# Three RMS norms in a two-block layer kernel: row factors applied behind the linear units, two norms merged into one factor, first units paired

## What is computed

```python
def rms_norm(x, g):
    y = x32 * lax.rsqrt(jnp.mean(x32 * x32, axis=-1, keepdims=True) + RMS_EPS)
    return (y * g.astype(jnp.float32)).astype(x.dtype)
...
    h = rms_norm(x, b_norm[j])                      # norm 1
    z = h @ w_in                                    # short_conv_mix
    c, b, u, g = jnp.split(z, 4, axis=-1)
    cu = c * u
    ...                                             # conv: 3 causal taps a channel
    y = b * conv * jax.nn.silu(g)
    x = x + y @ w_out
    x = rms_norm(x, final_norm)                     # norm 2
...
    h = rmsnorm(x, norm_mix_pre)                    # norm 3
    proj = jnp.einsum('bsd,de->bse', h, w_in)       # GLU, q, k, v, two gates
    ...
    mix = jnp.einsum('bsd,de->bse', merged, w_out)
    x = x + rmsnorm(mix, norm_mix_post)             # norm 4
    h = rmsnorm(x, norm_ffn_pre)                    # norm 5
    gu = jnp.einsum('bsd,df->bsf', h, w_ffn_up)
    gate, up = jnp.split(gu, 2, axis=-1)
    ff = jnp.einsum('bsf,fd->bsd', jax.nn.silu(gate) * up, w_ffn_down)
    x = x + rmsnorm(ff, norm_ffn_post)              # norm 6
```

## Time and profile before

| | us |
|---|---|
| median of 3 runs | 2272.75 |
| lowest, highest | 2270.09, 2278.52 |
| the profiled execution, its time | 2277.93 |
| the profiled execution, its span | 2276.2 |
| TensorE busy in the span | 2088.7 |
| DVE busy | 1405.7 |
| ACT busy | 992.6 |
| GpSimd busy | 279.1 |

### The profile page before, as it was taken

One profiled execution on the slowest core, in us unless ns is written; L12 is line 12 of the kernel. 1 busy time (PEld: TensorE's weight loads), 2 busy tenths in 40 slices (PEclk: granted clock), 3 DMA queues, 4 the chain that ended last, 5 costly groups with the idle time before them and its releaser, 6 DMA issues.

```text
span 2276.2 us, 43064 instructions
## 1 busy us (share of the span) xinstructions
PE 2088.7 (92%) x16752; PEld 1651.1 (73%) x16752; DVE 1405.7 (62%) x2178; ACT 992.6 (44%) x1742; POOL 279.1 (12%) x241
## 2 busy tenths in 40 slices
PE   6999999888888888989999999788989989999998
PEld 4877777677777766768788878566755757787876
DVE  7778888766666634465544555599765655434345
ACT  6666666455566653232322232411565334323233
POOL 4120000012222321000000000297000000000000
PEclk9999999899999988999999999999999999999998
DMA  4445555733332222323333333122211222333332
GB/s 115 125 138 170 174 170 171 200 71 87 69 78 69 69 76 59 94 69 101 88 97 93 92 101 92 47 74 65 84 38 38 80 68 75 100 93 92 93 88 79
DMA packets 395949, 215.16 MB, mean 95 GB/s; under 512 B 85136, under 2 KB 374312, under 8 KB 395816
## 3 DMA queue, kind: packets, MB, share of 16 engines
q1 hardware_dynamic: 395608, 213.18, 32.4%
q10 hardware_dynamic: 208, 0.06, 0.0%
HBM read 181.68 MB, written 31.52 MB: 94 GB/s over the span
## 4 chain that ended last, share of the span: by engine, by line
PE 69%; DVE 17%; ACT 8%; issue 5%; SPq 1%; DMA 1%; ACTq 0%; DVEq 0%
PE bank L1613 18%; PE bank L1614 17%; PE bank L1615 17%; PE bank L546 3%; DVE dconv L2104 3%; DVE w_lo L1834 2%; PE bank L523 1%; ACT w_hi L1337 1%; PE bank L554 1%; PE bank L455 1%; PE bank L497 1%; PE bank L469 1%; DVE tmp L1852 1%; PE bank L476 1%; DVE xh L1839 1%
## 5 line engine op out<-in xcount | busy, mean ns | idle before, releaser
L1613 PE MATMUL bank<-xl,w_hi 128*128 128x512 f32 x1680 | 670.6, 399 | 27.1 <-DVE xl L1839 9.9
L1614 PE MATMUL bank<-xl,w_lo 128*128 128x512 f32 x1680 | 661.4, 394 | 0.0
L1615 PE MATMUL bank<-xl,w_hi 128*128 128x512 f32 x1680 | 660.8, 393 | 0.0
L1337 ACT ACTIVATE w_hi<-w_raw 128x1024 fp32r<-128x1024 f32 x280 | 294.2, 1051 | 449.2 <-PE bank L1615 448.4
L1834 DVE TENSOR_TENSOR w_lo<-w_raw,w_hi 128x1024 fp32r<-128x1024 f32 x280 | 346.2, 1237 | 116.6 <-ACT w_hi L1337 107.6
L1613 PEld LDWEIGHTS bank<-xl,w_hi 128*128 128x128 f32 x1680 | 317.3, 189 | 129.3 <-issue 34.1
L1615 PEld LDWEIGHTS bank<-xl,w_hi 128*128 128x128 f32 x1680 | 317.6, 189 | 71.0
L1614 PEld LDWEIGHTS bank<-xl,w_lo 128*128 128x128 f32 x1680 | 317.9, 189 | 65.3
L1613 PE MATMUL bank<-xh,w_hi 128*128 128x512 f32 x480 | 202.1, 421 | 40.0 <-DVE w_lo L1834 23.7
L1614 PE MATMUL bank<-xh,w_lo 128*128 128x512 f32 x480 | 193.3, 403 | 0.0
L1615 PE MATMUL bank<-xh,w_hi 128*128 128x512 f32 x480 | 192.7, 402 | 0.0
(11 more groups left out here) (334 smaller groups left out, 3089.7 us busy)
## 6 DMA issues: line engine op xcount, KB each, us to landing
w_raw<-in_a_w_in SPq DMA_DIRECT2D x64, 512.0 KB, 4.3
w_raw<-in_b_w_in SPq DMA_DIRECT2D x64, 512.0 KB, 4.1
w_raw<-in_w_ffn_up SPq DMA_DIRECT2D x44, 512.0 KB, 3.9
w_raw<-in_w_in SPq DMA_DIRECT2D x36, 512.0 KB, 3.8
w_raw<-in_a_w_out SPq DMA_DIRECT2D x16, 512.0 KB, 4.1
w_raw<-in_b_w_out SPq DMA_DIRECT2D x16, 512.0 KB, 4.0
w_raw<-in_w_ffn_down SPq DMA_DIRECT2D x16, 512.0 KB, 4.1
d_g<-sq SPq DMA_DIRECT2D x16, 256.0 KB, 2.3
```

Source lines behind the costliest of these rows:

```text
L1337: A(w_hi[0:rows, slot, 0:nkb, 0:ncol], w_raw[0:rows, slot, 0:nkb, 0:ncol], ACT.Copy).then_inc(s_hi, 1)
L1613: mm(outp, wh, xlo, start=start, stop=False)
L1614: mm(outp, wl, xhi, start=False, stop=False)
L1615: return mm(outp, wh, xhi, start=False, stop=stop)
```

## The change

Norm 1: the high and low halves of x are made from x times the gain alone, in the eight units before the norm (`even` gets `hi` and `low`), and the factor r of each token is applied behind the units: r squared to the product c times u by way of c, r inside the sigmoid of g, r squared on g times b. The mean matmul stands behind the first convolution unit.

Norms 2 and 3: beside the sum of squares (`acc`), DVE sums the squares weighted with `square_gain` = final gain squared + 1e-6 (`acc2`). With an epsilon of 1e-12 its mean gives the product of both norms' factors at once, and the GLU's input is made with it and the product of both gains. The residual itself gets its final norm later: eight products `final_norm` in the first two GLU turns. The first two GLU units are interleaved part by part (`two_units`).

Norms 4 and 5: after the residual add, x times gain is split directly; the factor of norm 5 is applied in the FFN turns, in place of in front of them. Its squares are summed by TensorE between the matmuls of the first two FFN units, which are interleaved too.

The high and low panels of the second unit behind boundaries 2 and 3 are made ahead of the norm, and the first turns of two loops are written out. The core of the diff (each piece moved left by its common indentation):

```diff
@@ -1347,19 +1357,22 @@
-def norm(n, x, ready=None):
+def norm(n):
+
...
-    o(A(rstd[:, 0, :], bank[4][:], ACT.Ln, bias=eps[:, 0:1]))
-    A(rstd[:, 1, :], rstd[:, 0, :], ACT.Exp, scale=-0.5).then_inc(s_rs, 1)
+    if n == 3:
+        o(A(acc[:], bank[5][:], ACT.Ln, bias=eps[:, 0:1]))
+        A(acc[:], acc[:], ACT.Exp, scale=-0.5).then_inc(s_rs, 1)
+        return
+    e = 3 if n == 2 else 0
+    o(A(rstd[:, 0, :], bank[4][:], ACT.Ln, bias=eps[:, e:e + 1]))
+    ins = A(rstd[:, 1, :], rstd[:, 0, :], ACT.Exp, scale=-0.5)
+    if n in DEFERRED_SQUARED:
+        ins = A(rstd[:, 0, :], rstd[:, 0, :], ACT.Exp, scale=-1.0)
+    ins.then_inc(s_rs, 1)
@@ -1499,39 +1512,52 @@
-                act.wait_ge(s_sqa, 2 * t + (n * DK + u - 1))
+                if hi is not None:
+                    A(hi[:, 0, bass.ds(2 * t + u, 1), :], x[:, bass.ds(2 * t + u, 1), :], ACT.Copy,
+                      scale=col(gain, 2 * t + u)).then_inc(s_xhi, 1)
+                act.wait_ge(s_sqa, 2 * t + (squares(n) + u - 1))
                 A(sq[:, u, :], x[:, bass.ds(2 * t + u, 1), :], ACT.Square).then_inc(s_sq, 1)
...
-even(U_OUT1 + DK, DK // 2, xT2, 1)
-norm(1, None)
-for k in range(DK):
-    x_high(X_H2 + k, xl[2][:, 0, k, :], k % 2)
+even(U_OUT1 + DK, DK // 2, xT2, 1, hi=xl[2], gain="b_norm")
...
+            if first and u == 0:
+                norm(1)
...
-                sigmoid(gate3[:]).then_inc(s_sc, 1)
+                sigmoid(gate_z[:]).then_inc(s_sc, 1)
...
-norm(2, None)
-norm(3, xT2, lambda k: (s_xn, k + 1))
+ahead(U_GLU, 2, 0, 0)
+norm(2)
 for k in range(DK):
     x_high(X_H3 + k, xh[:, 0, k, :], k % 2)
+norm(3)
...
@@ -1579,27 +1605,39 @@
-norm(4, None)
-
-norm(5, xT2, lambda k: (s_mg, k + 1))
+ahead(U_FFN, 2, 0, 0)
+norm(4)
+
 for k in range(DK):
-    x_high(X_H4 + k, xl[0][:, 0, k, :], k % 2)
+    act.wait_ge(s_mg, k + 1)
+    A(xl[0][:, 0, k, :], xT2[:, k, :], ACT.Copy, scale=col("norm_ffn_pre_2", k)).then_inc(s_xhi, 1)
+    act.wait_ge(s_sqa, squares(5) + k - 1)
+    A(sq[:, k % 2, :], xT2[:, k, :], ACT.Square).then_inc(s_sq, 1)
+norm(5)
...
+    def ffn(t, first=False):
+        if not first:
+            ahead(base, 2, t, 0)
+        else:
+            ahead(base, 2, t, 1)
...
+        sigmoid(tmp[:, 1, :]).then_inc(s_us, 1)
...
@@ -1628,13 +1666,12 @@
-    if n not in SUMMED_BY_PE:
-        pe.wait_ge(s_sqa, (n + 1) * DK)
-        mm(bank[4][:], mean_d[:], acc[:], start=True, stop=True).then_inc(s_ms, 1)
+    if n == 2:
+        pe.wait_ge(s_sqb, DK + 1)
     else:
-        for k in range(DK):
-            pe.wait_ge(s_sq, n * DK + k + 1)
-            mm(bank[4][:], mean_d[:], sq[:, k % 2, :], start=k == 0, stop=k == DK - 1).then_inc(s_sqa, 1)
+        pe.wait_ge(s_sqa, squares(n + (n != 3)))
+    mm(bank[5 if n == 3 else 4][:], mean_d[:], acc2[:] if n == 2 else acc[:], start=True,
+       stop=True).then_inc(s_ms, 1)
@@ -1756,14 +1795,36 @@
-norm(1)
-    phase(base, 4, KB, xl[2], X_H2)
+    phase(base, 4, KB, xl[2], X_H2, then=None if half else lambda: norm(1))
 norm(2)
 norm(3)
-phase(U_GLU, 2, CT + 3 * AT // 2, xh, X_H3)
+
+def two_units(base, x, ready, total=None):
+
+    order = [(0, 0)]
+    for k in range(1, DK - 2):
+        order += [(0, k), (1, k - 1)]
+    order += [(0, DK - 2), (0, DK - 1)] + [(1, k) for k in range(DK - 3, DK)]
+    for u, k in order:
+        if k == 0:
+            pe.wait_ge(s_lo, base + u + 1)
+            pe.wait_ge(s_free[u], base // 2)
+        if u == 0:
+            pe.wait_ge(s_xlo, ready + k + 1)
+        last = three(bank[u][:], w_hi[:, u, k, :], w_lo[:, u, k, :], x[:, 0, k, :], x[:, 1, k, :],
+                     k == 0, k == DK - 1)
+        if k == DK - 1:
+            last.then_inc(s_unit, 1)
+        if total is not None:
+            if u == 0 and k:
+                total(k - 1)
+            elif (u, k) == (1, DK - 3):
+                total(DK - 1)
+two_units(U_GLU, xh, X_H3)
+phase(U_GLU, 2, CT + 3 * AT // 2, xh, X_H3, started=True)
@@ -1809,10 +1870,15 @@
-norm(5)
+def total_square(k):
+
+    pe.wait_ge(s_sq, squares(5) + k + 1)
+    mm(bank[4][:], mean_d[:], sq[:, k % 2, :], start=k == 0, stop=k == DK - 1).then_inc(s_sqa, 1)
+two_units(U_FFN, xl[0], X_H4, total_square)
...
-    phase(base, 2, n, xl[0], X_H4)
+    phase(base, 2, n, xl[0], X_H4, started=part == 0)
@@ -2021,9 +2080,20 @@
+            if low is not None:
+                part = bass.ds(2 * t + u, 1)
+                dve.wait_ge(s_xhi, 2 * t + (x0 + u + 1))
+                V.scalar_tensor_tensor(out=low[:, 1, part, :], in0=where, scalar=col(gain, 2 * t + u),
+                                       in1=low[:, 0, part, :].bitcast(F32), op0=ALU.mult,
+                                       op1=ALU.subtract).then_inc(s_xlo, 1)
...
+                if n == 2:
+                    dve.wait_ge(s_sqb, 2 * t + (u + 1))
+                    V.scalar_tensor_tensor(out=acc2[:], in0=sq[:, u, :],
+                                           scalar=square_gain[:, bass.ds(2 * t + u, 1)], in1=acc2[:],
+                                           op0=ALU.mult, op1=ALU.add).then_inc(s_sqb, 1)
...
-    even(U_OUT1 + half * DK, DK // 2, xT2, True, n=1 if half else None)
+even(U_OUT1, DK // 2, xT2, True)
+even(U_OUT1 + DK, DK // 2, xT2, True, n=1, low=xl[2], gain="b_norm", x0=X_H2)
...
-dve.wait_ge(s_xlo, X_H2)
-norm(1, "b_norm", split(X_H2, xl[2], DK), xT2, summed=True)
...
+o(V.tensor_tensor(both_gains[:], gain_f, gain_m, ALU.mult))
+o(V.tensor_tensor(square_gain[:], gain_f, gain_f, ALU.mult))
+o(V.tensor_scalar(square_gain[:], square_gain[:], RMS_EPS, None, ALU.add))
@@ -2056,7 +2130,8 @@
-        V.tensor_copy(c_sb[:], bank[0][:]).then_inc(s_free[0], 1)
+        dve.wait_ge(s_rs, 1 + NT)
+        V.tensor_tensor(c_sb[:], bank[0][:], rr_b, ALU.mult).then_inc(s_free[0], 1)
@@ -2070,23 +2145,32 @@
-        V.tensor_scalar(gate3[:], bank[0][:], CLAMP, None, ALU.max).then_inc(s_zc, 1)
-        dve.wait_ge(s_sc, ct + 1)
-        V.tensor_tensor(gate3[:], gate3[:], bank[0][:], ALU.mult).then_inc(s_free[0], 1)
+        o(V.tensor_tensor(gate_z[:], bank[0][:], r_b, ALU.mult))
+        V.tensor_scalar(gate_z[:], gate_z[:], CLAMP, None, ALU.max).then_inc(s_zc, 1)
+        V.tensor_tensor(gate3[:], bank[0][:], rr_b, ALU.mult).then_inc(s_free[0], 1)
         dve.wait_ge(s_free[0], 2 * t + (base // 2 + 2))
         o(V.tensor_tensor(gate3[:], gate3[:], conv3[:, 0, :], ALU.mult))
+        dve.wait_ge(s_sc, ct + 1)
+        o(V.tensor_tensor(gate3[:], gate3[:], gate_z[:], ALU.mult))
         w_low(n0 + 4, 0)
         dve.wait_ge(s_unit, n0 + 4)
         V.tensor_tensor(tmp[:, 0, :], gate3[:], bank[1][:], ALU.mult).then_inc(s_free[1], 1)
         x_low(t + (X_YC + KB * half), xl[half][:, 1, bass.ds(t, 1), :], xl[half][:, 0, bass.ds(t, 1), :], 0)
-    repeat(dve, KB, conv, o, 4)
+    repeat(dve, KB, conv, o, 6)
+    if half:
+        V.memset(acc2[:], 0.0).then_inc(s_sqb, 1)
-norm(2, "final_norm", lambda k, scaled: scaled(xT2[:, k, :]).then_inc(s_xn, 1), xT2,
-     summed=True)
+w_low(U_GLU + 1, 1)
-norm(3, "norm_mix_pre_2", split(X_H3, xh, DK), xT2)
+norm(2, lambda k: both_gains[:, k:k + 1], split(X_H3, xh, DK), xT2)
+
+def final_norm(k):
+
+    dve.wait_ge(s_rs, 3 + NT)
+    V.scalar_tensor_tensor(out=xT2[:, k, :], in0=xT2[:, k, :], scalar=col("final_norm", k), in1=acc[:],
+                           op0=ALU.mult, op1=ALU.mult).then_inc(s_xn, 1)
@@ -2115,6 +2200,8 @@
+    for k in range(4 * j, 4 * j + 4 if j < 2 else 0):
+        final_norm(k)
@@ -2205,36 +2292,57 @@
...
-    norm(n, gain, step, src, summed=True)
-residual(4, "norm_mix_post_2", mixed, s_mg)
-
-
-norm(5, "norm_ffn_pre_2", split(X_H4, xl[0], DK), xT2)
+        if low is not None:
+            for m in ([k - 2] if k >= 2 else []) + ([k - 1, k] if last else []):
+                low(m)
+def ffn_low(k):
+
+    dve.wait_ge(s_xhi, X_H4 + k + 1)
+    V.scalar_tensor_tensor(out=xl[0][:, 1, k, :], in0=xT2[:, k, :], scalar=col("norm_ffn_pre_2", k),
+                           in1=xl[0][:, 0, k, :].bitcast(F32), op0=ALU.mult,
+                           op1=ALU.subtract).then_inc(s_xlo, 1)
+w_low(U_FFN + 1, 1)
+dve.wait_ge(s_xn, DK)
+residual(4, "norm_mix_post_2", mixed, s_mg, ffn_low)
...
         n0 = 2 * t + base
-        w_low(n0 + 1, 1)
+        if not first:
+            w_low(n0 + 1, 1)
         dve.wait_ge(s_unit, n0 + 1)
-        V.tensor_scalar(rstd[:, 0, :], bank[0][:], CLAMP, None, ALU.max).then_inc(s_ug, 1)
+        dve.wait_ge(s_rs, 5 + NT)
+        V.tensor_tensor(rstd[:, 0, :], bank[0][:], r_ffn, ALU.mult).then_inc(s_free[0], 1)
+        dve.wait_ge(s_free[0], t + (base // 2 + 1))
+        V.tensor_scalar(tmp[:, 1, :], rstd[:, 0, :], CLAMP, None, ALU.max).then_inc(s_ug, 1)
         w_low(n0 + 2, 0)
+        o(V.tensor_tensor(rstd[:, 0, :], rstd[:, 0, :], r_ffn, ALU.mult))
         dve.wait_ge(s_us, t + (j0 + 1))
-        V.tensor_tensor(rstd[:, 0, :], rstd[:, 0, :], bank[0][:], ALU.mult).then_inc(s_free[0], 1)
```

(3 more changed lines are left out.)

102 lines of the change are left out of this document (61 added, 41 removed).

## The result

| | before | after |
|---|---|---|
| median of the runs | 2273.67 us (4 runs) | 2243.98 us (4 runs) |
| ratio, 95% interval | | 0.9869 [0.9845, 0.9893] |
| profiled execution (span) | 2277.93 (2276.2) | 2241.48 (2239.8) |

The forecast was 2243.0. On another chip the changed kernel took 2245.06 us against 2278.70: 0.9858 [0.9836, 0.9881].

What follows compares the result with a forecast made beforehand. TensorE, busy 92% of the span, was taken as the bound away from stage boundaries, so only its waits could be saved. Savings of 11.4 + 13.6 + 1.7 + 1.9 + 1.1 = 29.7 us gave a 2243 us median; profiled 2248, range 2236 to 2257.

Steps and rivals of the forecast that it cites:

- Boundary 1: Norm 1, before the convolution: splitting x no longer waits for rstd; saves 11.4 us (10.3 to 11.6).
- Boundary 2: Norms 2 and 3, before GLU: one chain goes; 13.6 us saved (11.5 to 15.5). E: end of the last unit before.
- Half clock: TensorE's restarts after idle run at half clock: 1.7 us added before GLU, 1.5 before the FFN.
- payback of 0.5 for the final norm: First two GLU turns: the eight final-norm products moved there cost 0.5 us in all (0 to 2.5).
- Rival (d): GLU stage: the final norm's eight products (5.4 us) come back whole, 2248 us; forecast with this included, 0.83.
- Boundary 3: Norms 4 and 5, before the FFN: mean matmuls between paired units make TensorE the bound; saves only 1.7 us (-2 to 4).
- the new wait: Third FFN unit: its panels are ready 4.0 us after the last mean matmul, of which two triples cover 1.4.
- Loops: 16 convolution turns save 1.9 us and 22 FFN turns 1.1 us; error on both together -5 to +5.
- Rival (a): Convolution and FFN turns: both added operations lie on each turn's chain, costing 47 us, so 2293 us, slower; chance 0.05.
- Rival (b): Convolution and FFN turns: a smaller loss of 0.5 us a turn, 19 us back, 2262 us; chance 0.08.
- Rival (c): GLU and FFN boundaries: clock stays at half through both paired stretches, 28 us instead of 3.2, 2268 us; chance 0.04.

Runs made afterwards that it cites:

- experiment 6: Changed kernel with final-norm products moved earlier (three ahead of the first GLU copy) and the last accumulator's memset ahead of the last FFN part: middle stretch 418.3, last 413.15 us.
- experiment 2: Changed kernel plus one unused VectorE product per FFN turn, in two kernels: ahead of the clamp 2259.79 us, behind the next weights' low panel 2243.35 us.

## Why the prediction was right

**Boundary 1**: forecast 11.4, measured 11.9 (13.7 less 16 turns of 0.11). All steps hold; the eight additions beside the output units hid (units 5.5 us apart, as before) and the granted clock stayed at 1.00 from 915 to 985 us. The difference is the mean product, 0.86 of stream and not 1.1, and the restart, which there was none of.

**Boundary 2**: forecast 13.6, measured 14.0. The restart was forecast at E+7.6 and came between E+7.8 and E+8.7, the third unit at E+22.5 in place of 21.8. Half clock cost 2.2 and not 1.7. The payback of 0.5 for the final norm did not show up: the sixth unit had lost 1.0 of the head start of 13.5, but at the attention it was whole again (14.1). Rival (d) falls, by the number; my reason, that the stage is VectorE's and has the same products as before, fits its 92.81 of 100 us and experiment 6. Why slightly more than the head start came through is not settled. The pairing, on which the text of this step leans, is worth 0.5.

**Boundary 3**: forecast 1.7, measured 4.3 at the third unit of the profiled run (others: E+33.5 and 32.7, so up to 5.7, but the latter lose 1.6 again to half clock in that unit). The structure was right: mean products between the parts, then the new wait. The mis-sized term is a mean product's price in the stream. I took 9.57 / 8 = 1.19 from the earlier trace rows. But there the first four of the sixteen entries, two products, ran at half clock (granted 0.50 over the first 3 us, first row below) and took 3.55 us where two products of the stream take 1.72: that is 1.8 of the excess of 2.7, and waits for squares are some 0.7. In a full stream at full clock a product is 0.86, eight of them 2.6 us less, which is about the whole error. So half clock was in part counted twice, in this price and in the 1.5 beside it.

```profile
1865.70:1868.70 3.00, 3.00 (x4) 1.27 (x5) 3.00 (x6) 1.26 (x2) 0.00 (x0) 0.50 0.00 0
1868.70:1875.30 6.60, 6.50 (x13) 1.89 (x12) 4.47 (x8) 3.15 (x5) 0.00 (x0) 0.96 0.00 0
```

**Loops**: 0.12 and 0.05 a turn were forecast, 0.11 and 0.065 measured. (The -0.3 that I gave for a clamp of 0.69 should have been 16 x -0.14 = -2.2.) Over the 22 FFN turns and their part ends the head start grew from 4.3 to 5.9 us. Behind the last turn 1.4 of it went back, which I had not looked at. The memset there is 0.6 of that (experiment 6); the kernel before had it at the same place, but there the low panel behind it started 8.66 us after the turn's first operation on VectorE, and now 9.88. Rival (a) was real as a mechanism (experiment 2: 0.72 a turn as soon as one more operation is on the chain) but this change stays clear of it by 0.8 us. Rival (b) falls, since both turns got shorter. Rival (c) falls: half clock ended after some 5.6 us at both places (4.0 in some profiles at boundary 3).

**Sum**: 29.7 forecast, 32 by stretches, and in medians 29.7 and 33.6 on two chips. That the first median met the forecast to a microsecond is partly luck: by stretch the terms were 2.6 short, most of it at boundary 3, and the other chip's medians differ by 3.9 more than the forecast.

## What to carry to other kernels

A factor that a norm applies can be moved behind the linear layer, and then the hole at the boundary shrinks to what the longest remaining chain is; look there for the wait that comes next (here a weight panel queued behind the factor's Ln and Exp) and take it out of the queue. Price an operation by the pace of a full stream at the clock that it will run at, not by entries that waited for inputs or ran at half clock. Interleaving two units bought 0.5 us here, and nothing where the next panel was late anyway. A run that gives the forecast number need not show its cause: follow the rows to the place where the time was gained.

## What I had not expected of the hardware

- A two-pass matmul of 128x512 costs the stream 0.86 us though its two entries read 1.02 together and the matmul behind it 0.79.
- Filling idle time with unused matmuls kept the granted clock at 1.00 through both restarts. Behind the same wait of 2.5 us the clock fell with them, and without them it fell in two profiles and stayed at 1.00 in four; what decides it is not shown.
- VectorE's products took 0.68 us each in the first GLU turn and 1.12 in the second, with GpSimd at its taps during the second alone. That GpSimd is the cause is likely and not tested. Moving products out of these turns did not shorten the stage.
